# Reading cached pages in their own order: the compression matmuls of a decoder trunk

## What is computed

```python
def compress(kv, w1, w2, pe):            # kv: (n, L, 2, N_KV, HEAD_DIM)
    blk = kv[:, :nb * BLK].reshape(n, nb, BLK, 2, N_KV, HEAD_DIM) + pe[:, :, None, :]
    hid = jax.nn.silu(jnp.einsum('nbpcgd,cpdh->nbcgh', blk, w1))
    return jnp.einsum('nbcgh,chd->nbcgd', hid, w2)

past_cmp = cmp_pool[page_table].reshape(n, past, 2, N_KV, HEAD_DIM)
```

## Time and profile before

| what | value |
|---|---|
| runs, device time | 1367.56, 1368.21, 1369.85 us; median 1368.21 |
| span of the profiled execution | 1372.2 us |
| TensorE busy (weight loads) | 1293.8 us, 94% (1180.1 us, 86%) |
| VectorE busy | 756.9 us, 55% |
| ScalarE busy | 431.1 us, 31% |
| GpSimd busy | 241.1 us, 18% |
| first FFN and its norm | 0 to some 518 us |
| granted TensorE clock, mean | 0.978 of full speed |

### The profile page before, as it was taken

The page is one execution under the profiler, slowest core; times in us unless marked ns, Lnnn a source line. Parts: engine busy times, 40 slices in busy tenths (PEclk is TensorE's granted clock), DMA queues, the critical chain, the costliest instruction groups (busy, mean ns, idle before and its releaser), DMA issues.

```text
span 1372.2 us, 29896 instructions
## 1 busy us (share of the span) xinstructions
PE 1293.8 (94%) x11917; PEld 1180.1 (86%) x11917; DVE 756.9 (55%) x1215; ACT 431.1 (31%) x813; POOL 241.1 (18%) x237
## 2 busy tenths in 40 slices
PE   6999999999999888999989999896999999999996
PEld 5999999999999877999956666695999999999994
DVE  4676487467737765334446666647344444344446
ACT  4322222223312225222235555316321222122224
POOL 1352044114404405000135334000000000000000
PEclk9999999999999999999989999898999999999998
DMA  4887176246625522322278665132532333333211
GB/s 140 223 214 178 57 207 194 70 133 182 186 79 171 160 55 63 66 63 78 73 237 263 205 226 170 36 89 80 162 102 85 105 97 102 107 107 102 82 61 65
DMA packets 216192, 173.95 MB, mean 127 GB/s; under 512 B 22947, under 2 KB 206418, under 8 KB 215700
## 3 DMA queue, kind: packets, MB, share of 16 engines
q1 hardware_dynamic: 209940, 155.64, 38.6%
q0 software_dynamic: 6144, 16.79, 3.7%
HBM read 168.44 MB, written 8.10 MB: 129 GB/s over the span
## 4 chain that ended last, share of the span: by engine, by line
PE 78%; DVE 11%; ACT 4%; DMA 3%; issue 3%; SPq 1%; POOL 0%; DVEq 0%; ACTq 0%
PE ps L770 44%; PE ps L899 8%; PE ps L826 7%; PE ps L796 4%; DVE dlo L1746 3%; PE ps L1255 2%; DMA draw<-in_ffa_down_dram 2%; DVE glo L1741 1%; PE ps L1226 1%; PE ps L1291 1%; PE ps L1271 1%; PE ps L1340 1%; PE ps L1003 1%; PE ps L1213 1%; ACT xh L1565 1%
## 5 line engine op out<-in xcount | busy, mean ns | idle before, releaser
L770 PE MATMUL ps<-xh,ghi 128*128 128x272 f32 x1872 | 395.1, 293 | 16.9 <-DVE xl L2010 14.2
L770 PE MATMUL ps<-xl,ghi 128*128 128x272 f32 x1872 | 388.8, 289 | 0.0
L770 PE MATMUL ps<-xh,glo 128*128 128x272 f32 x1872 | 387.4, 288 | 0.0
L770 PEld LDWEIGHTS ps<-xh,ghi 128*128 128x128 f32 x1872 | 299.5, 189 | 33.8 <-issue 17.6
L770 PEld LDWEIGHTS ps<-xl,ghi 128*128 128x128 f32 x1872 | 296.2, 190 | 0.0
L770 PEld LDWEIGHTS ps<-xh,glo 128*128 128x128 f32 x1872 | 295.3, 190 | 0.0
L1741 DVE TENSOR_TENSOR glo<-graw,ghi 128x1024 fp32r<-128x1024 f32 x117 | 144.0, 1231 | 108.0 <-ACT ghi L1392 105.8
L726 POOL COPY perm<-landing 128x1024 f32<-128x1024 f32 x64 | 140.9, 2215 | 304.0 <-DMA landing<-in_cache_cmp_kv_dram 303.9
L1816 DVE SCALAR_TENSOR_TENSOR x<-ps,x 128x544 f32<-128x544 f32 x176 | 126.8, 720 | 104.7 <-PE ps L826 104.3
L1875 DVE SCALAR_TENSOR_TENSOR yt<-ps,yt 128x512 f32<-128x512 f32 x88 | 60.6, 691 | 156.6 <-PE ps L899 156.6
L1392 ACT ACTIVATE ghi<-graw 128x1024 fp32r<-128x1024 f32 x117 | 122.7, 1049 | 30.9 <-PE ps L770 20.9
(11 more groups left out here) (344 smaller groups left out, 1492.5 us busy)
## 6 DMA issues: line engine op xcount, KB each, us to landing
landing<-in_cache_cmp_kv_dram SPq DMA_DIRECT2D x256, 128.0 KB, 2.5
page<-in_cache_sel_kv_dram SPq DMA_DIRECT2D x128, 128.0 KB, 4.9
page<-in_cache_sel_kv_dram POOLq DMA_DIRECT2D x128, 128.0 KB, 5.0
graw<-in_ffa_gate_dram SPq DMA_DIRECT2D x22, 512.0 KB, 4.9
graw<-in_ffa_up_dram SPq DMA_DIRECT2D x22, 512.0 KB, 4.1
draw<-in_ffa_down_dram SPq DMA_DIRECT2D x88, 128.0 KB, 2.8
graw<-in_w_in_dram SPq DMA_DIRECT2D x44, 256.0 KB, 3.3
graw<-in_ffb_gate_dram SPq DMA_DIRECT2D x22, 512.0 KB, 3.9
```

What stands on the lines that cost most here:

```text
L770: last = nc.tensor.matmul(out[:, h, 0:HALF], a[:, k, :], b[:, k, h * HALF:(h + 1) * HALF], start=(k == 0 and a is hi and b is xhi), stop=( ...
```

## The change

The landing buffers, the copies and their semaphores go. Pages are loaded straight into `group`, which has the size and place of `perm` but the order of the pages: 65 slots of 256 values in each partition, the 65th for the position embedding. The matmuls read their 130 columns out of it with a step of one slot, 1024 bytes, first 65 for one head, then 65 for the other. SP waits for `hid_in_psum` at the first quad of a group and for the transposes of the first tile at the first quad of all; TensorE waits for the loads themselves. SP's loop over the tiles that load pages is unrolled.

```diff
-        landing = [sb(f"landing{n}", [128, QUAD, KVW], F32, ffn) for n in range(2)]
+        sb("under_w1", [128, 2 * QUAD * KVW], F32, ffn)
         w1 = sb("w1", [128, 2, HD, HD], F32, ffn)
-        perm = sb("perm", [128, 2 * G, HD, PW], F32, ffn)
+        group = sb("group", [128, PW, KVW], F32, ffn)
...
-        def landing_loads(eng, b, first):
+        def group_loads(eng, at, first):
...
-                eng.dma_start(landing[b][:, k:k + 1, :], cache_cmp[0, DS(page, 1)].rearrange("o p c g d -> p o (c g d)")
-                              ).then_inc(dma_landing[b], 16)
+                eng.dma_start(group[:, at + k:at + k + 1, :], cache_cmp[0, DS(page, 1)].rearrange("o p c g d -> p o (c g d)")
+                              ).then_inc(dma_group, 16)
...
                     def pages(k):
                         if j is not None:
-                            free_from(permuted, j * 4 + (k - 1 + ONE))
-                            landing_loads(sp, k % 2, value(j * (4 * QUAD) + k * QUAD))
+                            quad = 4 * j + k
+                            if quad == 0:
+                                sp.wait_ge(xt_in_psum, KC)
+                                sp.wait_ge(small_in_psum, 1)
+                            elif quad % (GP // QUAD) == 0:
+                                sp.wait_ge(q["hid_in_psum"], quad * QUAD // GP)
+                            group_loads(sp, quad * QUAD % GP, quad * QUAD)
...
-                    with sp.Fori(first, last) as i:
+                    for i in range(first, last):
                         body(i, i + (4 * g - first))
...
-            pool.wait_ge(xt_in_psum, KC)
-            pool.wait_ge(small_in_psum, 1)
             pool.wait_ge(q["dma_first"], 16 * 5)
             for g in range(G):
-                pool.tensor_copy(perm[:, g:2 * G:G, :, GP], pe_sb[:])
-            for j in range(NB * NPG // QUAD):
-                g, at = divmod(j * QUAD, GP)
-                if g and at == 0:
-                    pool.wait_ge(q["hid_in_psum"], g)
-                pool.wait_ge(dma_landing[j % 2], (j // 2 + 1) * QUAD * 16)
-                pool.tensor_copy(perm[:, :, :, at:at + QUAD].rearrange("p x d a -> p a x d"),
-                                 landing[j % 2][:].rearrange("p a (x d) -> p a x d", d=HD)).then_inc(permuted, 1)
-
+                pool.tensor_copy(group[:, GP, :].rearrange("p (c g d) -> p c g d", c=2, g=G)[:, :, g, :], pe_sb[:]
+                                 ).then_inc(pe_placed, 1)
...
                             ps[c * HD:(c + 1) * HD, bank + h, 0:G * PW], w1[rows, c, d, :],
-                            perm[rows, c * G:(c + 1) * G, d, :], start=(d == 0), stop=(d == HD - 1))
+                            group[rows].rearrange("p a (c g d) -> p c d g a", c=2, g=G)[:, c, d],
+                            start=(d == 0), stop=(d == HD - 1))
...
-                        pe.wait_ge(permuted, (g + 1) * GP // QUAD + ONE)
+                        pe.wait_ge(dma_group, (g + 1) * GP * 16)
+                        pe.wait_ge(pe_placed, 2)
...
-                    pe.wait_ge(permuted, GROUPS * GP // QUAD + ONE)
+                    pe.wait_ge(dma_group, GROUPS * GP * 16)
...
-                dve.wait_ge(permuted, GROUPS * GP // QUAD + ONE)
                 dve.memset(csum[:], 0.0).then_inc(csum_step, 1)
```

## The result

The changed kernel takes 1444.45 us in the median (1443.70 to 1449.39) where the kernel before took 1367.88 beside it: a ratio of 1.0556 (95% interval 1.0530 to 1.0582). It is 5.6% slower. The forecast was 1355 us with a range of 1350 to 1414, so the time lies outside, on the side that had a chance of 0.48; the profiled execution has a span of 1441.9 us.

What follows compares the result with a forecast made beforehand. TensorE, with 78% of the chain and the compression blocks on it, was taken to bound the kernel. Span 1372.2 - 13.4 (copies) with loads and step at 0 gives 1358.8, less 4.0 to the median: 1355 us, range 1350 to 1414.

Steps and rivals of the forecast that it cites:

- What bounds the kernel: Whole kernel: TensorE carries 78% of the chain; compression blocks hide behind nothing, so longer rounds move the end as much.
- Part 1, the copies: Gate and up tiles, first FFN's end: without GpSimd's copies VectorE stops delaying TensorE; 13.4 us gained, bounds 9 and 16.
- the two late `draw` loads: Gate and up tiles: two of TensorE's 16 `dlo` waits, 1.2 and 0.8 us, come from late loads; not counted as gain.
- Part 2, the loads: Page loads straight into the group's buffer: no DMA work added, SP's new waits covered by margins; cost 0.
- Part 3, the strided operand: Compression matmuls: moving columns 1024 bytes apart cost a round nothing; taken at 0, other end 71 us.
- the nearest row: TensorE's weight load at L1347: 16 columns 520 bytes apart in 93 ns against 90.5 contiguous, so the step costs some 3 ns.
- the far end: Compression rounds: at VectorE's 1.92 ns per element a round takes 250 ns, 138 more; 512 rounds cost 71 us.
- The rule that I weighed: SBUF reads: full bandwidth needs two hits in a 16-byte line; here every column crosses to a new line.
- the shared path: Compression rounds: two streams on the same 64 partitions are served in turn, doubling a round; 57 us, 1412 us, chance 0.35.
- the first rival: Compression rounds: two streams share one read path and are served in turn; 1400 to 1414 us, chance 0.35.
- VectorE's price: Compression matmuls: every column costs what VectorE pays for wide steps; 71 us more, 1426 us, chance 0.07.
- Both effects together: Compression matmuls: streams served in turn and every column at VectorE's price; over 1480 us, chance 0.03.

Runs made afterwards that it cites:

- step series: Changed kernel, but each stretch of compression matmuls reads columns at another step: 4, 8, 16 bytes in full groups, 32, 256, 1008 in the last group's pieces; 1385.26 us.

## Why the prediction was wrong, point by point

- **What bounds the kernel:** right. TensorE and the compression's blocks are on the path, and 93 us of longer blocks came through to the end nearly whole.
- **Part 1, the copies:** right in place and mechanism, too small in size. The terms were 9.2 us in the tiles and 4.2 at the FFN's end. With columns side by side the third block starts 12.3 us earlier (383.82 against 371.53) and the last group's first piece 19.2 (490.60 against 471.44), so the tiles gave about 15. The traces say the same without the 4.2: TensorE starts the last product before the waits at the FFN's end at 474.17 us in before and at 459.53 with columns side by side, which leaves 14.6 for the tiles and 4.5 for the end. (Between 480 and 485 us, behind TensorE's longest wait, the granted clock was 0.50 in before, and in the same stretch with columns side by side it was 1.00; a step there takes 1.4 to 1.5 us in both, so this cost next to nothing.) In the tiles 2.0 us are the two late `draw` loads, which I had left in and which went too. Some 3 us more lie in no wait that the rows show, or in waits that lose more than the 0.16 us that were read off one example; which, is open.
- **Part 2, the loads:** right. No wait of TensorE in the tiles, no late page, no wait of SP for a group.
- **Part 3, the strided operand:** wrong, and this decided. Bounded by 0 and 71 us, taken at 0 by "the nearest row", the weight load of 16 columns. It measured 93 us: 62 as the price of a column in 16 bytes of its own, 31 by streams that hinder each other. Three things failed. The row was near in kind (TensorE's own read) but not in size: some 80 of its 93 ns don't depend on the columns, the price hides in the rest, and the 90.5 ns to which it was held were no measured load. The one row that could resolve the price per element, VectorE's 1.92 against 1.08, was kept as the far end: its 250 ns a round is close to the 233 to 242 that a step of 16, 32 or 1008 bytes costs (close in number; no run shows why two engines should pay alike). And the upper end was none, since neither row had several streams at once; that adds 60 ns a round, 31 us.
- **The rule that I weighed:** the Trainium skill, "SBUF — State Buffer", Specifications (TRN2), says that full bandwidth takes two hits in each 16-byte line. The step series agrees: 8 bytes, two columns to a line, 118 ns; 16 bytes, one, 233. I tied it to the shared path ("by the rule it is the first rival"), while here a stream alone already pays. The same page of the Trainium skill, Who interferes with whom, says that TensorE never waits for anyone; among its own streams it is slowed here (294 against 242 ns).
- **The rivals:** the first had sharing as the cause and a doubled round; the round is 2.6 times as long, and a stream alone already takes double. VectorE's price (1426 us, chance 0.07) was nearest: it had the mechanism, and 71 us where the step alone costs 62. With what the runs gave, 1368 - 20 + 62 + 31 = 1441 against the measured 1444; as the 62 and 31 are cut out of after's own blocks, this says only that nothing large is missing. Both effects together stood at "over 1480", because I took sharing for a second doubling.

## What to carry to other kernels

Before an operand's step is changed, count how many of its elements share 16 bytes: here a single one doubled a round on TensorE and lengthened a weight load of 64 columns by half (133 to 202 ns, in part hidden), while two cost a round 5 to 7%; copies that write single words took 1.8 times as long on ScalarE and GpSimd as those that write two. In this kernel a layout in pairs gives the matmuls most of what a full reordering gives (120 ns a round against 112). Price such a step by a row with many elements rather than by a short one of the same engine, and leave the upper end open where two streams will read the same partitions. Where one engine holds up another, try shorter instructions: cutting GpSimd's copies in four, with more busy time in all, gained 0.8%, and beginning `csum` later brought it to 1.0%.

## What the runs showed that I had not expected

- The price is a step and not a slope: 118 ns a round at 8 bytes, 233 at 16, 242 at 1008.
- Two streams on the same partitions take 294 ns a round at 1024 bytes and 295 at 256, but 242 at 1008, with another distance between them; alone, a pair takes 209 to 228 ns at any step from 16 bytes on. Weight loads show a like extra: 250 ns at 1024 bytes against 202 at 1008.
- The weight loads of `w1`, unchanged and side by side, take 161 ns in the mean beside wide streams in after, against 132 in the kernel before.
- ScalarE, in the same copies, is no faster than GpSimd: 2115 and 2215 ns with single words, 1203 and 1248 in pairs.
